# Latent attention projected for all heads in one passage ahead of the heads, in place of a slot in each head

## The reference

```python
qm = (rms_norm(cq, mla_q_norm_w[i]) @ mla_w_uq[i]).reshape(b, s, MLA_HEADS, MLA_QK_DIM)      # 512 -> 8 x 96
q_nope = qm[..., :MLA_NOPE_DIM]                                                              # 64
q_pe = apply_rope(qm[..., MLA_NOPE_DIM:], positions, MLA_ROPE_DIM)                           # 32
kv = (rms_norm(ckv, mla_kv_norm_w[i]) @ mla_w_ukv[i]).reshape(b, s, MLA_HEADS, MLA_NOPE_DIM + MLA_V_DIM)
k_nope = kv[..., :MLA_NOPE_DIM]                                                              # 256 -> 8 x 64
v_m = kv[..., MLA_NOPE_DIM:]                                                                 # 256 -> 8 x 64
k_pe = apply_rope(krope[:, :, None, :], positions, MLA_ROPE_DIM)
mo = causal_attention(q_full, k_full, v_m, MLA_QK_DIM ** -0.5)
```

## Time and profile before

| what | before |
|---|---|
| median of 3 runs | 2068.82 us (2067.64 to 2069.63) |
| the profiled execution's own time | 2068.48 us |
| its span, first to last instruction | 2066.7 us |
| PE, PEld, DVE, ACT, POOL busy | 2021.5, 1659.3, 1041.1, 883.6, 1104.0 us |
| matmuls in the trace | 9533 |
| mean granted TensorE clock | 0.996 of full |

### The profile page before, as it was taken

How to read it: one execution, slowest core, us unless ns; L and a number is a source line. 1 busy time by engine, 2 the same in 40 slices (tenths; PEclk the granted TensorE clock), 3 DMA queues, 4 the chain that set the end, 5 groups by cost and what they waited for, 6 DMA issues and landing times.

```text
span 2066.7 us, 31024 instructions
## 1 busy us (share of the span) xinstructions
PE 2021.5 (98%) x9533; PEld 1659.3 (80%) x9533; DVE 1041.1 (50%) x1791; ACT 883.6 (43%) x1548; POOL 1104.0 (53%) x1456
## 2 busy tenths in 40 slices
PE   7999999999999999999999899999999999999997
PEld 5877888888788888888888687888887888888886
DVE  6446767776754433322143567777756543333111
ACT  5444554554643323233344345554555343222332
POOL 6554454344555555557765543444445646555674
PEclk9999999999999999999999999999999999999999
DMA  6332232223553333333352322222245433333232
GB/s 223 104 106 79 68 89 78 80 71 92 173 168 102 99 95 99 94 111 97 99 166 79 99 79 83 67 77 77 68 133 173 147 92 102 96 97 95 81 94 87
DMA packets 363902, 212.75 MB, mean 103 GB/s; under 512 B 23926, under 2 KB 349628, under 8 KB 363068
## 3 DMA queue, kind: packets, MB, share of 16 engines
q1 hardware_dynamic: 347838, 173.87, 29.5%
q10 hardware_dynamic: 15998, 38.04, 5.2%
HBM read 191.40 MB, written 20.45 MB: 103 GB/s over the span
## 4 chain that ended last, share of the span: by engine, by line
issue 40%; POOL 39%; PE 20%; POOLq 1%; ACT 0%; DMA 0%; DVE 0%; SPq 0%; ACTq 0%; DVEq 0%
POOL w_lo L525 38%; PE proj L563 6%; PE proj L564 6%; PE proj L565 6%; POOLq L528 0%; POOLq L530 0%; DMA raw<-in_w_out 0%; PE flip L908 0%; ACT y_out L1376 0%; POOL rope_t L516 0%; PE score L927 0%; PE score L575 0%; POOL freq L499 0%; POOLq L525 0%; DVE mix_lo L1812 0%
## 5 line engine op out<-in xcount | busy, mean ns | idle before, releaser
L525 POOL TENSOR_TENSOR w_lo<-raw,w_hi 128x256 fp32r<-128x256 f32 x1408 | 1098.3, 812 | 938.6 <-ACT w_hi L945 937.8
L563 PE MATMUL proj<-h_hi,w_hi 128*128 128x512 f32 x1632 | 650.6, 399 | 6.2 <-DVE mqT L1411 6.2
L565 PE MATMUL proj<-h_hi,w_lo 128*128 128x512 f32 x1632 | 636.4, 390 | 0.0
L564 PE MATMUL proj<-h_lo,w_hi 128*128 128x512 f32 x1632 | 635.7, 389 | 0.0
L945 ACT ACTIVATE w_hi<-raw 128x1024 fp32r<-128x1024 f32 x352 | 369.9, 1057 | 267.1 <-PE proj L565 71.5
L563 PEld LDWEIGHTS proj<-h_hi,w_hi 128*128 128x128 f32 x1632 | 306.1, 188 | 75.3 <-issue 10.0
L564 PEld LDWEIGHTS proj<-h_lo,w_hi 128*128 128x128 f32 x1632 | 306.3, 188 | 65.4 <-issue 4.1
L565 PEld LDWEIGHTS proj<-h_hi,w_lo 128*128 128x128 f32 x1632 | 305.9, 187 | 65.2
L563 PE MATMUL proj<-hid_hi,w_hi 128*128 128x512 f32 x352 | 137.6, 391 | 0.0
L565 PE MATMUL proj<-hid_hi,w_lo 128*128 128x512 f32 x352 | 137.1, 389 | 0.0
L564 PE MATMUL proj<-hid_lo,w_hi 128*128 128x512 f32 x352 | 137.0, 389 | 0.0
(11 more groups left out here) (318 smaller groups left out, 3106.6 us busy)
## 6 DMA issues: line engine op xcount, KB each, us to landing
raw<-in_w_in SPq DMA_DIRECT2D x232, 256.0 KB, 3.0
raw<-in_w_gate_up SPq DMA_DIRECT2D x176, 256.0 KB, 2.9
...
```

Source lines behind the costliest of these rows:

```text
L525: ins = g.tensor_tensor(w_lo[s][:, cols], raw[s % 2][:, cols], w_hi[s][:, cols].bitcast(F32), ALU.subtract)
L563: mm(o, hi[:, c:c + width], rh, start=start and k == 0, stop=False)
L564: mm(o, hi[:, c:c + width], rl, start=False, stop=False)
L565: ins = mm(o, lo[:, c:c + width], rh, start=False, stop=stop and k == n - 1)
```

## The change

Latent queries, keys and values are projected once per layer, for all heads, in stage Z; heads have five slots and not six.

- The host lays the weights out anew: mla_w_uq as all heads' 64 plain columns and then all rope columns, mla_w_ukv as all key columns and then all value columns.
- Z has nine slots: Q of head 0 (into bank score0), three slots of query tiles (two rope tiles with four heads each, four plain tiles with two heads each, into score1, proj0, flip0, flip1, att, proj1), a gate, a slot of key tiles (four tiles, 6 matmuls each), a slot of value tiles, K, V. A gate slot moves from Z to A, where the two half slots of the rope key become one.
- ACT copies the plain query tiles to gate_in and the key tiles to k_nope; DVE ropes the two rope tiles at once, for all heads, into gate_in.
- The values are projected token-wise (the latent is the stationary operand, the weights move), so they need no flip. High and low halves lie side by side in one tile mv with 128 columns for each head, and the latent attend is two products for each key block; ACT copies the lower 64 rows of the result out of PSUM and DVE adds the two halves.
- In a head ACT copies the next head's query rows, DVE its rope rows and key rows (`query_rows`, `latent_rows`). The Q slot stands between the scores of the two maps, the K slot is whole, the second gate slot is cut in two. On DVE the K rope moves before causal_low(1, 1), query_low before causal_low(1, 0), and causal_low(0, 1) behind the normalising of p_b.
- The seven heads with a successor are written out on every engine.
- In the last head gate_in holds the queries until they are copied, so `load_gates` moves behind the exps of d2; att_square moves ahead of four outs_high.
- The tables of the latent rope cover all four groups of 32 partitions: `rope_rows` loops over six entries and not three, four copies each.

```diff
+                slot(l, "Z", 0, 0, *whole(w_in, l, C_DQ))
+                slot(l, "Z", 0, 1, *two_tiles(l, HEADS * NOPE))
+                slot(l, "Z", 0, 2, *two_tiles(l, 0))
+                slot(l, "Z", 0, 3, *two_tiles(l, 2 * P))
+                slot(l, "Z", 0, 4, *gate(l, GATES_Z))
+                slot(l, "Z", 0, 5, *wide(l, 0))
+                slot(l, "Z", 0, 6, *wide(l, HEADS * NOPE))
+                slot(l, "Z", 0, 7, *whole(w_in, l, C_DK))
+                slot(l, "Z", 0, 8, *whole(w_in, l, C_DV))
...
+            def latent_attend(l, h):
+                pe.wait_ge(flip_read.sem, flip_read.at(l, "B", h, 4))
+                pe.wait_ge(att_read.sem, att_read.at(l, "B", h))
+                for j in range(NT):
+                    cols = slice(k_off(j), k_off(j) + SEQ - j * P)
+                    mm(att[:, j * P:SEQ], mv[:, h, j, :], pt_hi[:, cols], start=j == 0, stop=False)
+                    ins = mm(att[:, j * P:SEQ], mv[:, h, j, :], pt_lo[:, cols], start=False, stop=j == NT - 1)
+                ins.then_inc(att_full.sem, 1)
             def flip_values(l, h):
-                for k, (src, copied) in enumerate(((vT, v_copied), (kvT, kv_copied))):
-                    pe.wait_ge(copied.sem, copied.at(l, "B", h, 1))
...
+            def query_tiles(l, s, banks, frees):
+                for n in range(2):
+                    unit(l, "Z", 0, s, banks[n], frees[n], QT, cq_rhs, first=n * QT * P).then_inc((tile_done, slot_done)[n].sem, 1)
...
+            def key_tiles(l, s, banks):
...
+                    pe.wait_ge(uq_copied.sem, uq_copied.at(l, "Z", 0, n + 1))
...
+                    product([(b[:, :], w_hi[w][:, c[k]], w_lo[w][:, c[k]], ckv_hi[:, k, :], ckv_lo[:, k, :])
+                             for k in range(KVT)]).then_inc((tile_done if n < 3 else slot_done).sem, 1)
+            def value_tiles(l, s, banks):
...
+                    pe.wait_ge(k_nope_copied.sem, k_nope_copied.at(l, "Z", 0, t + 1))
...
+                    product([(b[:, :], ckv_hi[:, k, c], ckv_lo[:, k, c], w_hi[w][:, 512 * k:512 * k + 512], w_lo[w][:, 512 * k:512 * k + 512])
+                             for k in range(KVT)]).then_inc((tile_done if t < 3 else slot_done).sem, 1)
...
+            def head(l, h):
+                n = h + 1
                 def w(s):
-                    return ring("B", s, e)
-                unit(l, "B", h, 0, 0, (gate_copied, gate_copied.at(l, "B", h)), KD, h_rhs, w=w(0)).then_inc(slot_done.sem, 1)
+                    return ring("B", s, h)
+                unit(l, "B", h, 0, 0, (gate_copied, gate_copied.at(l, "B", h)) if h else (diff_ready, diff_ready.at(l, "B", 0, 2)),
+                     KD, h_rhs, w=w(0)).then_inc(slot_done.sem, 1)
                 pe.wait_ge(qk_split.sem, qk_split.at(l, "B", h, 2))
                 causal_scores(l, h, 1)
                 causal_flip(l, h, 0, 0)
-                pe.wait_ge(ssq_read.sem, ssq_read.at(l, "B", h))
-                latent_units(l, "B", h, 1, w(1), n, (diff_ready, diff_ready.at(l, "B", n)), (v_copied, v_copied.at(l, "B", n, 1)))
+                unit(l, "B", h, 1, 1, (ssq_read, ssq_read.at(l, "B", h)) if h else (v_copied, v_copied.at(l, "B", 0, 1)),
+                     KD, h_rhs, w=w(1)).then_inc(slot_done.sem, 1)
                 causal_flip(l, h, 0, 1)
                 causal_scores(l, h, 2)
-                unit(l, "B", h, 2, 1, (mla_ready, mla_ready.at(l, "B", n, 1)), KD, h_rhs, w=w(2)).then_inc(slot_done.sem, 1)
-                unit(l, "B", h, 3, 0, (kv_copied, kv_copied.at(l, "B", n, 1)), KD, h_rhs, w=w(3)).then_inc(slot_done.sem, 1)
-                causal_attend(l, h, 0, mv_hi, mv_lo)
-                unit(l, "B", h, 4, 1, (diff_ready, diff_ready.at(l, "B", n, 1)), 4, h_rhs, stop=False, w=w(4))
+                unit(l, "B", h, 2, 0, (v_copied, v_copied.at(l, "B", n, 1)), KD, h_rhs, w=w(2)).then_inc(slot_done.sem, 1)
+                latent_attend(l, h)
+                unit(l, "B", h, 3, 1, (diff_ready, diff_ready.at(l, "B", n, 1)), KD, h_rhs, w=w(3)).then_inc(slot_done.sem, 1)
                 causal_flip(l, h, 1, 0)
-                unit(l, "B", h, 4, 1, None, 4, lambda k: h_rhs(k + 4), first=4 * P, start=False, w=w(4)).then_inc(slot_done.sem, 1)
+                unit(l, "B", h, 4, 0, (gate_copied, gate_copied.at(l, "B", h, 1)), 4, h_rhs, stop=False, w=w(4))
                 causal_flip(l, h, 1, 1)
-                unit(l, "B", h, 5, 0, (gate_copied, gate_copied.at(l, "B", h, 1)), KD, h_rhs, w=w(5)).then_inc(slot_done.sem, 1)
+                unit(l, "B", h, 4, 0, None, 4, lambda k: h_rhs(k + 4), first=4 * P, start=False, w=w(4)).then_inc(slot_done.sem, 1)
                 latent_scores(l, n)
-                causal_attend(l, h, 1, v_hi, v_lo)
+                causal_attend(l, h)
                 flip_values(l, n)
...
-                unit(l, "Z", 0, 1, 0, (mla_ready, mla_ready.at(l, "B", 0)), KD, h_rhs).then_inc(slot_done.sem, 1)
-                unit(l, "Z", 0, 2, 1, (v_copied, v_copied.at(l, "B", 0, 1)), KD, h_rhs).then_inc(slot_done.sem, 1)
-                pe.wait_ge(pair_lo.sem, pair_lo.at(l, "A", 0, QT + KVT))
-                latent_units(l, "Z", 0, 3, ring("Z", 3), 0, (gate_copied, gate_copied.at(l, "Z", 0, 1)), (diff_ready, diff_ready.at(l, "B", 0, 1)))
-                unit(l, "Z", 0, 4, 1, (mla_ready, mla_ready.at(l, "B", 0, 1)), KD, h_rhs).then_inc(slot_done.sem, 1)
-                unit(l, "Z", 0, 5, 0, (kv_copied, kv_copied.at(l, "B", 0, 1)), KD, h_rhs).then_inc(slot_done.sem, 1)
+                unit(l, "Z", 0, 0, score[0], (exp_done, exp_done.at(l, "B", 0)), KD, h_rhs).then_inc(slot_done.sem, 1)
+                pe.wait_ge(pair_lo.sem, pair_lo.at(l, "A", 0, QT))
+                query_tiles(l, 1, (score[1], proj[0]), (None, (mla_ready, mla_ready.at(l, "A", 0, 1))))
+                query_tiles(l, 2, (flip[0], flip[1]), ((flip_read, flip_read.at(l, "B", 0)), None))
+                query_tiles(l, 3, (att, proj[1]), ((att_read, att_read.at(l, "B", 0)), (gate_copied, gate_copied.at(l, "A", 0, 3))))
+                unit(l, "Z", 0, 4, 0, (mla_ready, mla_ready.at(l, "Z", 0, 2)), KD, h_rhs).then_inc(slot_done.sem, 1)
+                key_tiles(l, 5, (flip[0], flip[1], att, proj[1]))
+                value_tiles(l, 6, (flip[0], flip[1], att, proj[1]))
+                unit(l, "Z", 0, 7, 0, (gate_copied, gate_copied.at(l, "Z", 0, 1)), KD, h_rhs).then_inc(slot_done.sem, 1)
+                unit(l, "Z", 0, 8, 1, (mv_split, mv_split.at(l, "Z", 0, 4)), KD, h_rhs).then_inc(slot_done.sem, 1)
                 pe.wait_ge(ssq_read.sem, ssq_read.at(l, "B", 0))
+                pe.wait_ge(diff_ready.sem, diff_ready.at(l, "B", 0, 1))
...
+            def query_rows(l, h):
+                act.wait_ge(uq_copied.sem, uq_copied.at(l, "Z", 0, h // 2 + 1))
+                copy(mqT[0:NOPE, :], gate_in[half_of(h), h // 2, :]).then_inc(mq_copied.sem, 1)
...
                 exps(l, "B", h, 0, "m", p_a, MLA_SCALE)
-                split_ahead(l, "B", h, 0, e)
+                split_ahead(l, "B", h, 0, h)
+                query_rows(l, n)
                 causal_high(l, h, 0, 0)
                 act.wait_ge(flip_full.sem, flip_full.at(l, "B", h))
                 exps(l, "B", h, 1, "d1", p_b, DIFF_SCALE)
-                split_ahead(l, "B", h, 1, e)
+                split_ahead(l, "B", h, 1, h)
                 causal_high(l, h, 0, 1)
-                out_kv(l, n)
-                act.wait_ge(flip_full.sem, flip_full.at(l, "B", h, 5))
+                act.wait_ge(flip_full.sem, flip_full.at(l, "B", h, 4))
                 exps(l, "B", h, 2, "d2", p_a, DIFF_SCALE)
-                split_ahead(l, "B", h, 2, e)
-                split_ahead(l, "B", h, 3, e)
-                copy_gate(l, "B", h, 3, 0, 0)
-                split_ahead(l, "B", h, 4, e)
+                split_ahead(l, "B", h, 2, h)
+                query_high(l, n)
+                copy_gate(l, "B", h, 2, 0, 0)
+                split_ahead(l, "B", h, 3, h)
+                att_mla(l, h)
                 store_gate(l, "B", h, 0, h * 2 + GATES_B)
-                att_mla(l, h, h % 2 if isinstance(h, int) else e)
                 causal_high(l, h, 1, 0)
-                query_high(l, n)
-                split_ahead(l, "B", h, 5, e)
+                split_ahead(l, "B", h, 4, h)
                 causal_high(l, h, 1, 1)
                 key_high(l, n)
-                copy_gate(l, "B", h, 5, 0, 1)
+                copy_gate(l, "B", h, 4, 0, 1)
...
-                for b in range(2):
-                    act.wait_ge(gate_stored[b].sem, gate_stored[b].at(l, "L"))
-                act.wait_ge(gate_n_stored.sem, gate_n_stored.at(l, "N", 0, 16))
-                for e in range(2):
-                    load_gates(l, 0, e)
...
+                for b in range(2):
+                    act.wait_ge(gate_stored[b].sem, gate_stored[b].at(l, "L"))
+                act.wait_ge(gate_n_stored.sem, gate_n_stored.at(l, "N", 0, 16))
+                act.wait_ge(mla_ready.sem, mla_ready.at(l, "B", h, 1))
```

(40 more changed lines are left out.)

290 lines of the change are left out of this document (169 added, 121 removed).

## The result

The changed kernel takes 2023.41 us (median of 4 runs, 2022.88 to 2025.65) against 2068.83 (4 runs, 2067.64 to 2069.63): ratio 0.978, 95% interval 0.977 to 0.980, **45.4 us faster**. The forecast was 2027.7, with a range of 2019 to 2038. The profiled execution took 2023.66 us, its span is 2021.8.

What follows compares the result with a forecast made beforehand. PE's list of matmuls was taken to bound the kernel (busy 2021.5 of 2066.7 us). Terms 17.5 + 14.6 - 71.4 - 3.6 + 1.8 = -41.1 us gave 2027.7 us, range 2019 to 2038.

Steps and rivals of the forecast that it cites:

- the main case: Whole kernel: the forecast itself, 2023 to 2030 us, chance 0.53.
- All five terms: Z of layer 0 +17.5 us, Z of layer 1 +14.6, 14 heads -71.4, last heads -3.6, start +1.8.
- the mqT wait: In each of 14 heads, PE's wait on the mqT rope behind the latent slot goes: 0.2 us.
- The attend: In each head, the latent attend runs two products per key block instead of three: 0.62 us less.
- the latent slot: In each of 14 heads, the slot with 12 + 6 matmuls goes: 4.24 us less.
- The flips for a_sq exchange: End of each head: four kvT flips go, 0.44 us, but 0.4 comes back as PE's wait for a_sq.
- the 0.1 wait for V: End of Z: PE arrives after V and the scores and waits 0.1 us for DVE's key work and V's copy.
- This takes for granted that the waits go: Z: waits of 1.97 us for the gate copy and 1.6 for mqT go, and the latent slot's half clock.
- Rival (d): Every head: PE's K slot waits for a late Q rope on DVE; slower, 2080 us; chance 0.03.
- PE then waits as much as now for pt_lo: Last head of each layer: PE's wait for pt_lo stays at 0.5 us a layer.
- a wait of about 2 us at the cross flip: Start: sign that the 12 new rope_rows copies lengthen PE's cross flip wait, 0.41 us before, by 1.8.
- rival (c): Start is dearer: copies meet POOL, or the 2 us wait brings half clock; 3 to 7 us more; chance 0.15.

Runs made afterwards that it cites:

- the experiment: Kernel before, with the product of the values' low remainder and the probabilities left out of every head's latent attend (4 matmuls of 12); 2059.21 us.
- two experiments from both sides: Changed kernel with four more transposes of vT behind flip_values, 2024.16 us; changed kernel with 14 heads' ones product behind the next slot's first three matmuls, 2016.38 us.
- the norm-first experiment: Kernel before, with ACT's part of the ckv norm in Z moved ahead of the weight slot conversion that waits for its load; 2061.02 us.

## Why the prediction was right, point by point

- **Forecast and range.** 2027.7 against 2023.4: the main case, which reached from 2023 to 2030, at its lower edge. All five terms have the right sign. Four were too careful, by 4.5 us in all, of which the heads are 2.6; the start was 0.7 us dearer than forecast. That the last heads and the start come so near is in part luck, as told below.
- **A head: 5.1 forecast, 5.24 measured** (45.39 to 40.15 in layer 0; over all 14 it is 74.0, 5.29 each). The mis-sized term is the mqT wait: I took the printed 0.2; in PE's starts above, the step from the d2 scores to the next slot shrank from 1.98 to 1.60, so 0.38. The attend gave 0.65 in that head (0.62 forecast and in the experiment), the latent slot 4.14 net (4.24). The flips for a_sq exchange, 0.44 against 0.4, is shown by two experiments from both sides. The sign that I gave for it, a_sq some 16 times at 0.4, came as 14 times 0.23 and twice 0.7 in print.
- **Z: 52.7 forecast, 52.3 measured**, because a slot takes 5.44 us and not 5.5; the 0.1 wait for V did not come. "This takes for granted that the waits go" held, and the norm-first experiment shows what it rested on: nearly all of the gate_out wait beyond 0.9 us was a matter of order on ACT.
- **Does DVE keep up?** The K slot comes 2.4 us after the Q rope (2 forecast), the flips 4.1 after the maps (3.2). The two new copies in a head take 0.84 and 0.86 us; the fastest of the first kind took 0.51. All 32 of them ran beside POOL, so what one costs undisturbed is not shown, but the loss is 0.33 us at least, and it is hidden. Rival (d) had no foothold. In head 1 the copies end at 260.07 and 260.94, 0.28 us behind the POOL instructions that ran when they started (259.79 and 260.66), and the one of 0.51 in Z ends at 184.44, as far behind one that ends at 184.16. The rule cited in the prediction (the Trainium skill, "SBUF — State Buffer", "Who interferes with whom") has the later of the two wait for the whole instruction of the other; the trace agrees. By these rows a copy lost up to 0.58 us, an estimate that takes the 0.28 for its undisturbed time.
- **Last heads: 3.6 forecast, 4.6 measured**, a step that failed in its reasons. The d2 scores came 0.4 and 1.06 us sooner (0.4 and 0.8), a_sq gave 0.47 and 0.43 (0.6 each, too much). "PE then waits as much as now for pt_lo" is wrong: that wait went, 0.5 each, with the order of the outs_high copies. Moving the loads without it gains nothing. The two errors have opposite signs, so the total looks better than its reasons.
- **The start: 1.8 forecast, 2.5 in the profile.** The 1.8 is right for DVE (4.64 us of copies against 2.88), and PE's step to the first cross flip is as much longer (12.91 against 11.15). The rest is 0.7 of a longer wait for mem_n ahead of it. That need not be the change's: over the kernel before and its six versions this wait runs from 0.8 to 1.8 us. The sign that I gave, a wait of about 2 us at the cross flip, did not come; it was 0.5, because PE at half clock came late itself, and behind that only 0.6 to 1.0 us of the copies could be recovered. Part of rival (c) happened, without its cause: the half clock comes in kernels that lack the copies.
- **Unrolling** is free on PE; its 4 us in the kernel before come by way of the late load, as far as the profile shows.
- **Where the other 37.5 us come from**, in the numbers above: 24 matmuls fewer a layer (10.8), sixteen attends (16 x 0.62 = 9.9), fourteen mqT waits in heads (5.3), the waits for mqT and gate_out that Z still had with the norm first (5.0), the last heads' own 3.4, which are again order and not projections; together 34.4. The start takes 2.5 of it back. The rest, 5.6 us, was not taken apart.
